# Weight sums begun every six tiles, two reorderings in the feed-forward: one decoder layer on one core

## The reference, cut to what matters

```python
def run_layer(x, l, conv_prefix, s0, mk, mv):
    m, conv_state, s_new = token_mix(rms_norm(x, norm_mix_g[l]), ...)   # conv heads and gated linear attention
    x = x + m
    x = x + cross_attn(rms_norm(x, norm_xa_g[l]), mk, mv, w_xq[l], w_xo[l])
    h = rms_norm(x, norm_ffn_g[l])
    x = x + jnp.square(jax.nn.relu(h @ w_up[l])) @ w_down[l]
    return x, conv_state, s_new
# memory_kv makes mk, mv for the prompt; a last rms_norm follows for both token groups
```

## Time and profile before

| | |
|---|---|
| three runs | 1506.53, 1507.82, 1508.70 us (median 1507.82) |
| the profiled execution | 1508.38 us, its span 1506.6 us |
| PE busy | 1387.1 us, 92% of the span |
| DVE, ACT, POOL busy | 1031.5, 742.9, 298.6 us |
| mean granted TensorE clock | 0.964 of full |
| DMA | 268.24 MB moved, mean 178 GB/s; SP's queue 48.2%, POOL's 12.9% of the 16 engines |
| adds into `sums` by POOL | 32 of 1 MB, median 15.8 us from issue to landing |

### The profile page before, as it was taken

How to read it: one execution, slowest core, us unless ns; L and a number is a source line. 1 busy time by engine, 2 the same in 40 slices (tenths; PEclk the granted TensorE clock), 3 DMA queues, 4 the chain that set the end, 5 groups by cost and what they waited for, 6 DMA issues and landing times.

```text
span 1506.6 us, 25755 instructions
## 1 busy us (share of the span) xinstructions
PE 1387.1 (92%) x10477; PEld 1350.3 (90%) x10477; DVE 1031.5 (68%) x1403; ACT 742.9 (49%) x1062; POOL 298.6 (20%) x240
## 2 busy tenths in 40 slices
PE   7999678599879999999988999999997999999997
PEld 7889678599769999998987999999987999999997
DVE  5629595588543355562276878787898888598884
ACT  7551124234733253341336647484754757475663
POOL 6647249222353221110430000000000000000000
PEclk9999899799989999999998999999999999999997
DMA  8898899888838451158223555555554555466652
GB/s 328 250 245 207 212 237 160 210 211 225 188 121 261 135 189 43 43 194 297 91 94 122 177 182 172 186 175 182 183 168 127 181 183 169 155 198 207 196 161 57
DMA packets 138117, 268.24 MB, mean 178 GB/s; under 512 B 16073, under 2 KB 30729, under 8 KB 136593
## 3 DMA queue, kind: packets, MB, share of 16 engines
q1 hardware_dynamic: 121104, 233.04, 48.2%
q0 software_dynamic: 16896, 33.56, 12.9%
HBM read 254.26 MB, written 79.41 MB: 221 GB/s over the span
## 4 chain that ended last, share of the span: by engine, by line
PE 66%; DMA 15%; DVE 7%; ACT 5%; POOL 3%; issue 3%; SPq 1%; DVEq 0%; ACTq 0%; POOLq 0%
PE ps L2199 32%; DMA sums<-in_wt 8%; PE ps L1628 6%; PE m L2199 6%; PE ps L2035 5%; DMA w_raw<-in_wt 5%; PE ps L1741 4%; PE ps L2140 3%; POOL w_split L869 2%; PE m L1709 1%; PE ps L2069 1%; PE ps L1988 1%; PE m L1948 1%; DVE u_op L2798 1%; DVE comb_a L2807 1%
## 5 line engine op out<-in xcount | busy, mean ns | idle before, releaser
L1741 PE MATMUL ps<-a_op,w_split 128*128 128x344 f32 x1440 | 239.6, 326 | 28.9 <-POOL w_split L869 14.1
L1741 PEld LDWEIGHTS ps<-a_op,w_split 128*128 128x128 f32 x1440 | 231.6, 192 | 31.2 <-ACT gate_in L1107 16.0
L869 POOL TENSOR_TENSOR w_split<-w_raw,w_split 128x512 fp32r<-128x512 f32 x114 | 159.1, 1453 | 448.1 <-ACT w_split L971 448.0
L1469 ACT ACTIVATE comb_a<-raw_a 128x1024 fp32r<-128x1024 f32 x148 | 153.7, 1052 | 111.3 <-DMA raw_a<-in_wt 71.5
L2199 PE MATMUL ps<-d_op,comb_a 128*128 128x258 f32 x1512 | 193.5, 285 | 12.2 <-DVE comb_a L2807 6.3
L2199 PEld LDWEIGHTS ps<-d_op,comb_a 128*128 128x128 f32 x1512 | 187.2, 190 | 14.2 <-DVE comb_a L2807 9.3
L2199 PE MATMUL ps<-u_op,comb_a 128*128 128x258 f32 x1512 | 190.5, 284 | 9.3 <-DVE u_op L2798 5.4
L2199 PEld LDWEIGHTS ps<-u_op,comb_a 128*128 128x128 f32 x1512 | 185.7, 190 | 10.6 <-DVE u_op L2798 5.6
L2807 DVE TENSOR_TENSOR comb_a<-raw_a,comb_a 128x1024 fp32r<-128x1024 f32 x148 | 179.5, 1218 | 5.3 <-ACT comb_a L1469 5.3
L2412 DVE SCALAR_TENSOR_TENSOR ps<-conv_in,par,ps 128x1024 f32<-128x1024 f32 x103 | 133.0, 1291 | 3.3
L971 ACT ACTIVATE w_split<-w_raw 128x1024 fp32r<-128x1024 f32 x58 | 60.8, 1050 | 102.1 <-DMA w_raw<-in_wt 94.0
(11 more groups left out here) (362 smaller groups left out, 2360.8 us busy)
## 6 DMA issues: line engine op xcount, KB each, us to landing
raw_a<-sums SPq DMA_DIRECT2D x167, 256.0 KB, 2.9
raw_a<-in_wt SPq DMA_DIRECT2D x129, 256.0 KB, 2.9
sums<-in_wt POOLq DMA_DIRECT2D x32, 1024.0 KB, 15.8
w_raw<-in_wt SPq DMA_DIRECT2D x59, 512.0 KB, 4.5
sums<-in_wt SPq DMA_DIRECT2D x16, 1024.0 KB, 10.3
sums<-sums SPq DMA_DIRECT2D x16, 1024.0 KB, 7.2
raw_c<-sums SPq DMA_DIRECT2D x43, 256.0 KB, 2.9
raw_b<-sums SPq DMA_DIRECT2D x42, 256.0 KB, 2.8
```

What stands on the lines that cost most here:

```text
L869: gp.tensor_tensor(split(t, slot)[:, 1, part, :], src, split(t, slot)[:, 0, part, :].bitcast(F32), ALU.subtract).then_inc(w_low_done, 1)
L1469: act.activation(pair_of(j)[0][:, 0:n_, 0], pair_of(j)[1][:, 0:n_, 1], ACT.Copy).then_inc(comb_high, 1)
L1741: last = pe.matmul(PS[0][:, b, 0:CB], w_split[:, p % 2, wp, k, :], a_op[:, k, xp, b * CB:(b + 1) * CB], start=(k == 0 and j == 0), stop=(k ...
```

## The change

Three edits. First, the groups of sums begin every six tiles instead of every three (`SUM_START`), S3 one tile behind S1; the copies that wait for adds stand 7 and 12 tiles behind the group's start instead of 3 and 6, the adds at 2, 3, 8 and 13 instead of 1, 1, 4 and 7. POOL issues the adds ahead of the tile's low part instead of behind it. The last group begins at tile 57; its last copy and add fall to steps 2 and 3 of the feed-forward, for which both engines get calls there. Second, on VectorE, in the first "down" step of a group, the low part that stood between `add_first` and `add_second` goes behind `add_second`. Third, at step 45 TensorE makes the norm sums behind product 1 instead of product 4, and ACT does `final_norm` between its first and second high part instead of at the step's end.

```diff
--- before.py
+++ after.py
@@ -100,7 +100,7 @@
 LOW_PAIRS = [(PAIRS[s - 1][-2:] if s else []) + PAIRS[s][:-2] for s in range(LAST_STEP)]
 LOW_PAIRS[-1] = LOW_PAIRS[-1] + PAIRS[LAST_STEP - 1][-2:]
 SUMS = ("S1", "S2", "S3", "S4")
-T_SUM = T_IN - 1
+SUM_START = [T_IN - 1 + 6 * g for g in range(2 * FG)]
 OLD_LOADS = [4 + sum(t % 2 == r for t in range(T_IN, T_SPLIT)) for r in range(2)] + [4, 4]
 F_SQUARES = 19 + XO_HALVES
 E_SQUARES, E_SUMS = F_SQUARES + KT, F_SQUARES + KT - 1
@@ -640,16 +640,17 @@
 
             def copy_sums(t):
                 for g in range(2 * FG):
-                    at_ = t - T_SUM - 3 * g
+                    at_ = t - SUM_START[g]
                     if at_ == 0:
                         if g >= 3:
                             wait_added(sp, g - 3, 4)
                         sp.dma_start(sum_of(g, "S1"), blocks(g, "A22")).then_inc(sums_copied[g % 3], 16)
+                    elif at_ == 1:
                         sp.dma_start(sum_of(g, "S3"), blocks(g, "A11")).then_inc(sums_copied[g % 3], 16)
-                    elif at_ == 3:
+                    elif at_ == 7:
                         wait_added(sp, g, 2)
                         sp.dma_start(sum_of(g, "S2"), sum_of(g, "S1")).then_inc(sums_copied[g % 3], 16)
-                    elif at_ == 6:
+                    elif at_ == 12:
                         wait_added(sp, g, 3)
                         sp.dma_start(sum_of(g, "S4"), sum_of(g, "S2")).then_inc(sums_copied[g % 3], 16)
 
@@ -773,6 +774,8 @@
             for s in range(N_ST):
                 for j in PAIRS[s]:
                     load_pair(j)
+                if s < KT:
+                    copy_sums(T_SPLIT + s)
                 for i, at_step in enumerate(SCALE_STEPS):
                     if s == at_step + 1:
                         sp.wait_ge(y_ready, 2 * (i + 1))
@@ -871,15 +874,17 @@
 
             def add_sums(t):
                 for g in range(2 * FG):
-                    at_ = t - T_SUM - 3 * g
-                    if at_ == 1:
+                    at_ = t - SUM_START[g]
+                    if at_ == 2:
                         wait_copied(gp, g, 2)
                         gp.dma_start(sum_of(g, "S1"), blocks(g, "A21"), accum_op=ALU.add).then_inc(sums_added[g % 3], 16)
+                    elif at_ == 3:
+                        wait_copied(gp, g, 2)
                         gp.dma_start(sum_of(g, "S3"), blocks(g, "A21"), accum_op=ALU.add).then_inc(sums_added[g % 3], 16)
-                    elif at_ == 4:
+                    elif at_ == 8:
                         wait_copied(gp, g, 3)
                         gp.dma_start(sum_of(g, "S2"), blocks(g, "A11"), accum_op=ALU.add).then_inc(sums_added[g % 3], 16)
-                    elif at_ == 7:
+                    elif at_ == 13:
                         wait_copied(gp, g, 4)
                         gp.dma_start(sum_of(g, "S4"), blocks(g, "A12"), accum_op=ALU.add).then_inc(sums_added[g % 3], 16)
 
@@ -889,8 +894,8 @@
                 for m in range(CT):
                     if p == T_IN + I_C + 2 * m + 1:
                         gate_product(m)
+                add_sums(p + 2)
                 lo(p + 2, p % 2)
-                add_sums(p + 2)
                 if p == T_IN + I_C + 2:
                     decay_tree()
                 if 2 * CT <= p - T_IN - I_C < 2 * CT + 4:
@@ -940,7 +945,9 @@
 
             assert T_OUT % 2 == 1
             for t in range(T_OUT + 2, T_SPLIT):
+                add_sums(t)
                 lo(t, t % 2)
+            for t in range(T_SPLIT, T_SPLIT + KT):
                 add_sums(t)
 
 
@@ -1580,6 +1587,8 @@
                 comb_top(next(pairs, N_PAIR))
                 if s == 0:
                     norm_half(1)
+                if s == NORM_STEP:
+                    final_norm()
                 comb_top(next(pairs, N_PAIR))
                 if kind == "up":
                     relu_first(s)
@@ -1588,8 +1597,6 @@
                     comb_top(j)
                 if s in SUM_STEPS:
                     final_square(2 * (s - SUM_STEPS[0]) + 1)
-                if s == NORM_STEP:
-                    final_norm()
             end_square(LAST_STEP - 1)
             for b, (c0, w) in enumerate(END_BLOCKS):
                 c_ = slice(HT + c0, HT + c0 + w)
@@ -2220,17 +2227,17 @@
                 else:
                     for i in range(4):
                         product(s, i)
+                        if s == NORM_STEP and i == 1:
+                            wait_c11_read(pe, s - 1)
+                            pe.wait_ge(c_step, 5 * (s - 1) + 4)
+                            pe.wait_ge(squares_summed, E_SUMS)
+                            idle = SETS[(s + 1) % 2]
+                            half_sums((idle[0], idle[2]), lambda b: f_sum[:, b, :])
                 product(s, 4)
                 if s == 0:
                     pe.wait_ge(ps_free, T_SPLIT)
                     pe.wait_ge(squares_summed, 19 + XO_HALVES)
                     half_sums((PS[1][:, 0, :], PS[1][:, 1, :]), lambda b: acc[:, HT + Q * b:HT + Q * (b + 1)])
-                if s == NORM_STEP:
-                    wait_c11_read(pe, s - 1)
-                    pe.wait_ge(c_step, 5 * (s - 1) + 4)
-                    pe.wait_ge(squares_summed, E_SUMS)
-                    idle = SETS[(s + 1) % 2]
-                    half_sums((idle[0], idle[2]), lambda b: f_sum[:, b, :])
                 product(s, 5)
                 product(s, 6)
 
@@ -2949,8 +2956,11 @@
                 if s == SWITCH + KT // 2:
                     factor_rest(1, 3)
                 add_first(s)
-                low_pair(next(pairs, N_PAIR))
+                if not (after_up and p == 0):
+                    low_pair(next(pairs, N_PAIR))
                 add_second(s)
+                if after_up and p == 0:
+                    low_pair(next(pairs, N_PAIR))
                 if after_up and p:
                     hidden_low(s - 1, "all")
                 if s in SUM_STEPS and s > SUM_STEPS[0]:
```

## The result

The changed kernel takes 1448.97 us (median of 4 runs, 1447.22 to 1453.93) against 1507.17 of the kernel before on the same chip (1501.46 to 1508.70): ratio 0.9626, interval 0.9590 to 0.9662. It is faster, and 11.6 us slower than the predicted 1437.4: inside the range of 1427 to 1456, outside the 1430 to 1446 that the prediction held likeliest. Its profiled execution took 1447.22 us with a span of 1445.5, 61.1 less than the 1506.6 of before, where 70.4 were forecast.

What follows compares the result with a forecast made beforehand. It held that SP's waits for POOL's adding DMAs delay weight loads queued behind them and so stall TensorE. Terms summed to 70.4 us off 1508.4, giving 1438.0, or 1437.4 at the median; range 1427 to 1456, likeliest 1430 to 1446.

Steps and rivals of the forecast that it cites:

- two rivals (1450 and 1452): Halves crowded by slow weight loads: 1450, chance 0.10; POOL or VectorE the next bound in the input projection: 1452, chance 0.13.
- input projection: Three TensorE stalls and slow matmuls go, 46.0 us; 1.2 gained from a smaller stall, 1.0 lost to new waits.
- halves: Second projection's half tiles: copies and adds at tiles 57 to 60 delay weight loads, 3.0 us lost.
- decode stall: TensorE's 14.25 us wait for the decode state's load goes, with 1.0 of slow matmuls: 15.2 us gained.
- output projection and attention: Sums of later groups now lie here; forecast to change nothing.
- feed-forward and end: Low parts gain 7.6 us, norm sums 5.4, the copy and add in steps 2 and 3 lose 1.0.
- At 11.4 us a tile and more nothing there changes: Claim that sums moved into the output projection and attention cost no time there.
- The rival that DMA is the bound: In the input projection DMA, not waits, is the bound: about 1470 us, chance 0.04.
- two things to separate: Input projection: are waits or full DMA the limit; forecast 48 of 68 us a group, DMA 0.7 full.
- Feed-forward, copy and add: Last copy and add in steps 2 and 3 delay block loads: 0 to 4 us, 1.0 lost taken.
- Low parts and norm sums: Feed-forward: eight TensorE gaps of 0.95 us go, 7.6; the wait and slow matmuls at step 46 go, 5.4.

Runs made afterwards that it cites:

- e7: The kernel before with groups of sums every six tiles instead of three and nothing else: 1487.19 us, ratio 0.9914.
- e1: The changed kernel with the moved low part and moved norm sums put back, so the sums edit alone: 1459.25 us, ratio 0.9718.
- e4: The changed kernel with other group starts, so that no add is issued at tiles 46 to 48: 1427.70 us, ratio 0.9522.
- e8: e6 with the sample keys' load also moved behind the first keys and values: 1427.92 us, ratio 0.9517.
- e6: e4 with the last group begun at tile 53 instead of 56, ending the sums before the feed-forward: 1426.92 us, ratio 0.9512.
- e5: The changed kernel with the 4 MB sample keys' load moved behind the first keys and values at tile 49: 1436.45 us, ratio 0.9574.
- e10: e8 with group 4 begun a tile earlier (36) and the last group a tile later (54): 1421.48 us, ratio 0.9483.

## Why the prediction was right in sign and 11.6 us off

The measured 1448.97 lies in the range, but near the prices of two rivals (1450 and 1452), and neither of them came: the input projection has 2.5 us of new waits and the halves lost 2.4. That the range held is luck. It was stretched for those two, and the loss came from a stretch that the prediction had put at nothing.

The ledger of the profiled executions, in us gained:

| term | forecast | trace | from |
|---|---|---|---|
| input projection | 46.2 | 54.7 | its first row to the first `v_tok,k_in` row: 330.4, now 275.7 |
| decode stall | 15.2 | 14.3 | from there to the sample tokens' product: 32.4, now 18.1 |
| output projection and attention | 0 | -13.3 | stage table, before rounding |
| halves | -3.0 | -2.4 | stage table |
| feed-forward and end | 12.0 | 7.7 | stage table, before rounding |
| sum | 70.4 | 61.1 | spans |

**The step that failed** is the sentence "At 11.4 us a tile and more nothing there changes". It judged the output projection by the weight loads, which have a tile's time of slack. The small loads of the same queue were not looked at. ScalarE's and VectorE's timelines of before have the keys' high and low part:

```profile
552.29 0.63 ACT L1342 ACTIVATE k_op<-k_raw 128x512 fp32r<-128x512 f32 x1 [3.64 <-DMA k_raw<-out_mk]
```

```profile
552.96 0.69 DVE L2617 TENSOR_TENSOR k_op<-k_raw,k_op 128x512 fp32r<-128x512 f32 x1 [2.15 <-ACT k_op L1342]
```

ScalarE waited for this load already, and the low part ended at 553.65, 0.24 us before TensorE took it at 553.89. There was no gap to see, and no slack either: whatever the load lost would be lost by TensorE. In the changed kernel the load took 17.6 us for 4.1, and TensorE stood 13.16 us.

**Input projection.** The mechanism was right. Two sizes were low. The idle time fell by 46.0 us, not 41.0: small gaps of before between the large ones (3.06 before 252.74, 0.83, 0.50) went too, and I had not listed them, and the 2.46 before 96.24 went whole, not by 1.2. The matmuls became faster by 8.7 us, not 5.2. Of the difference, 1.6 lie behind that same gap of 2.46, where 216 took 35.80 and not 34.24, which the sum left out. Behind the third stall the first rows lost some 2.1 and not 1.6 (16 took 3.58 us at 285.49, 1.95 undisturbed). New waits came on VectorE, 2.5 us for 1.0, but that size is near by luck: not the taps but the stretched copy held it. The rival that DMA is the bound falls: its share is 0.64, forecast 0.7. In 160 to 200 us it is 0.96 and TensorE still has no gap. The step "two things to separate" named the right test and then left it undone; by e7 the spacing alone gives that stage.

**Decode stall.** Right, mechanism and size.

**Halves.** Nearly right: one gap instead of several, behind a weight load of 11.94 us. TensorE's timeline and the chain in time order:

```profile
682.77 14.78 PE L2147 MATMUL ps<-a_op,w_split 128*128 128x258 f32 x120 [2.13 <-POOL w_split L872]
```

```profile
668.25 11.94 DMA w_raw<-in_wt
```

**Feed-forward, copy and add.** The gap alone used up the range of 0 to 4 us. It was 3.97, and the 57 matmuls behind it, from 801.62 to 811.47, took 9.85 us where 0.127 us each make 7.24: another 2.6, so 6.6 in place of 1.0 in that execution (e1's has a gap of 2.41 there). I had looked at the loads and not at what ScalarE has queued behind a load it waits for.

**Low parts and norm sums.** The gaps of 7.6 and 2.77 us went as said. In time the two edits alone gave 2.6 and 3.5 us, below the forecast 7.6 and 5.4; taken out of the changed kernel (e1) they cost some 14, with an interval of 7 to 20. Whether a count of gaps in one trace was too good a price isn't settled, nor what would take the rest back. By the trace, the feed-forward's 6.1 us are 7.6 and 5.4 less 6.6, that is 6.4, so in that one execution the sum closes.

**The clock of the sum.** 9.3 of the 11.6 us are in the ledger. Of the other 2.3, 1.8 lie between the profiled execution, the fastest of its four runs, and the median, and the rest in the step from the profiled execution to the median of before.

## What to carry to other kernels

Before background transfers are moved, list the loads with no slack in the stretch that they are moved to, small ones above all, and for each what is issued ahead of it in its own queue; one megabyte ahead of the keys came with 5.6 us of gap and slower matmuls, four that adds had slowed with 15.5 (13.16 and 2.3). Spreading a burst and putting off its waits are different cures: in this kernel the first sufficed where a tile of 11.4 us hid the wait, and the second was needed in the halves and ahead of the keys. To every forecast gap of 3 us or more add what the matmuls behind it lose (1.5 to 2.5 us here), and let an effect of a few us stand only when repeated timing shows it.

## What the runs showed of the hardware

- A stall costs more than its idle time. Behind gaps of 3.00, 3.11, 3.26, 13.16, 13.40 and 21.14 us (e4, e8, e6, the changed kernel, e1, e7) the same 24 matmuls took 5.46, 5.46, 4.55, 5.30, 4.94 and 4.44 us in place of 2.98; behind one of 1.22 or 0.78 (e5, e10) they took 3.07 and 3.08. The loss was no larger behind the long gaps than behind those of 3 us. In the changed kernel the mean granted clock of these matmuls (495.73 to 501.03 us) is 0.53, close to the lower level, 1.2 GHz; before the gap and from 501.03 on it is full.
- From 470 to 480 us of the changed kernel, POOL's adds had 70.5% of the engines' time and SP's queue 39.3% (time of packets of both, overlapping). Each moved 1.31 MB: an accumulated byte took some 1.8 times the engine time of a loaded one. Over the whole span the page has 13.4% for POOL's 33.56 MB and 49.9% for SP's 233.04, a ratio of 1.9.
- A copy of 128 x 16 on VectorE took 4.5 to 4.6 us in three kernels, 1.07 to 1.24 in five and 0.18 in the one without adds (rows above).
